# An encoder trunk with routed experts: first three expert passes' rows loaded by token number, a 16-row tile moved up, one entry norm on ScalarE

## The reference, cut to what matters

```python
def hier_moe(h, w_group, w_router, w_gate, w_up, w_down):
    g_probs = softmax(t @ w_group); g_sel = argmax(g_probs)          # 1 of 4 groups
    top_p, top_i = lax.top_k(softmax(e_logits of that group), 2)     # 2 of its 4 experts
    weights = g_w * top_p / sum(top_p)
    hid = silu(t @ w_gate[e]) * (t @ w_up[e]) * gate[e]              # 16 experts, 256 wide
    y = sum over e of hid @ w_down[e]
```

## Time and profile before

| | us |
|---|---|
| median of three runs (lowest, highest) | 1149.74 (1149.23, 1150.93) |
| the profiled execution, device time | 1149.54 |
| its span | 1147.8 |
| TensorE busy | 1060.4 (92%) |
| VectorE / ScalarE / GpSimd busy | 447.5 / 262.4 / 238.5 |
| moved by DMA | 200.88 MB |
| chain that ended last, by engine | PE 79%, DVE 12%, issue 3%, ACT 2%, DMA 2%, POOL 1% |

### The profile page before, as it was taken

The page is one execution under the profiler, slowest core; times in us unless marked ns, Lnnn a source line. Parts: engine busy times, 40 slices in busy tenths (PEclk is TensorE's granted clock), DMA queues, the critical chain, the costliest instruction groups (busy, mean ns, idle before and its releaser), DMA issues.

```text
span 1147.8 us, 16421 instructions
## 1 busy us (share of the span) xinstructions
PE 1060.4 (92%) x6544; PEld 672.0 (59%) x6544; DVE 447.5 (39%) x807; ACT 262.4 (23%) x527; POOL 238.5 (21%) x232
## 2 busy tenths in 40 slices
PE   4999999999999999978999998989998978999992
PEld 4979979989988877753333332454444443333331
DVE  6400314224226540046133125657547745132217
ACT  5132143124224411020011111314214500011111
POOL 5324214305314533003000005510000002000005
PEclk8999999999999999998999998989999997999997
DMA  7232224115115111376799887130003067899946
GB/s 298 74 121 82 66 79 132 55 31 170 55 37 166 37 74 74 147 293 260 283 355 384 354 369 255 49 146 1 1 1 147 1 246 303 333 362 350 381 193 233
DMA packets 34837, 200.88 MB, mean 175 GB/s; under 512 B 4352, under 2 KB 4480, under 8 KB 25808
## 3 DMA queue, kind: packets, MB, share of 16 engines
q1 hardware_dynamic: 21168, 151.26, 34.5%
q10 hardware_dynamic: 8864, 31.63, 7.9%
q0 software_dynamic: 4736, 17.04, 4.0%
HBM read 303.59 MB, written 28.44 MB: 289 GB/s over the span
## 4 chain that ended last, share of the span: by engine, by line
PE 79%; DVE 12%; issue 3%; ACT 2%; DMA 2%; POOL 1%; POOLq 0%; ACTq 0%; DVEq 0%
PE ps L842 30%; PE ps L1076 15%; PE ps L1095 7%; PE ps L967 4%; PE ps L1200 4%; PE ps L1142 3%; PE ps L848 2%; DVE arena L2058 2%; PE ps L1064 2%; DVE arena L2055 2%; PE ps L910 1%; PE ps L1053 1%; PE ps L1014 1%; ACT arena L1510 1%; PE ps L1160 1%
## 5 line engine op out<-in xcount | busy, mean ns | idle before, releaser
L842 PE MATMUL ps<-x_hi,ring_r 128*128 128x264 f32 x1024 | 191.9, 288 | 2.6 <-DVE xT L1550 2.5
L2138 POOL TENSOR_TENSOR ring_r<-ring,ring_r 128x1024 fp32r<-128x1024 f32 x56 | 134.9, 2422 | 266.2 <-ACT ring_r L1292 266.2
L842 PEld LDWEIGHTS ps<-x_hi,ring_r 128*128 128x128 f32 x1024 | 161.1, 190 | 3.3 <-issue 2.9
L1076 PE MATMUL ps<-arena,xT 128*32 128x512 f32 x864 | 158.0, 600 | 0.0
L1076 PE MATMUL ps<-ring,xT 128*32 128x512 f32 x672 | 143.8, 602 | 5.9 <-DVE xT L1550 5.9
L842 PE MATMUL ps<-xT_r,ring_r 128*128 128x264 f32 x512 | 146.6, 286 | 0.0
L1550 DVE TENSOR_TENSOR xT<-ps,gains 128x512 f32<-128x512 f32 (+1 forms) x76 | 47.0, 660 | 186.9 <-PE ps L1064 177.1
L842 PE MATMUL ps<-ring_r,x_hi 128*128 128x512 f32 x320 | 100.5, 395 | 0.0
L842 PEld LDWEIGHTS ps<-xT_r,ring_r 128*128 128x128 f32 x512 | 97.4, 190 | 0.1
L1095 PE MATMUL ps<-arena 128*32 128x512 f32 x624 | 87.3, 595 | 4.3 <-ACT arena L1424 4.3
L1292 ACT ACTIVATE ring_r<-ring 128x1024 fp32r<-128x1024 f32 x56 | 57.9, 1054 | 119.5 <-PE ps L842 70.8
(11 more groups left out here) (264 smaller groups left out, 1573.1 us busy)
## 6 DMA issues: line engine op xcount, KB each, us to landing
arena<-in_w_gu SPq DMA_DIRECT2D x22, 2048.0 KB, 14.9
ring<-in_w_gu SPq DMA_DIRECT2D x20, 2048.0 KB
arena<-in_w_down SPq DMA_DIRECT2D x36, 1024.0 KB
arena<-in_w_gu POOLq DMA_DIRECT2D x18, 2048.0 KB
ring<-in_w_gu POOLq DMA_DIRECT2D x14, 2048.0 KB
arena<-in_w_down POOLq DMA_DIRECT2D x26, 1024.0 KB
ring<-in_w_ret SPq DMA_DIRECT2D x48, 512.0 KB, 3.7
ring<-in_w_ret_out SPq DMA_DIRECT2D x16, 512.0 KB, 4.9
```

The source lines that it names most:

```text
L842: last = mm(dst, a_parts[x], b_parts[y], start=(start and n == 0), stop=(stop and n == 2))
L1076: last = mm(ps[cols, b, :], xgT[:, k % 2, c, cols], by_row(gu(j))[:, c, :], start=(c == 0), stop=(c == KT - 1))
L2138: G.tensor_tensor(w_lo[slot][:, m], w_raw[slot][:, m], w_hi[to][:, m], ALU.subtract).then_inc(lo_made, 1)
```

## The change

- **Rows by token number.** For passes 0, 1 and 2 the one-hot matrices (now three, `slots_of_pass`) are multiplied by a column of token numbers instead of by the rows (`tokens_of`, five products of one column). ScalarE turns the result into integers `token_i`, and GpSimd fetches the 128 rows with one indirect DMA from `token_rows`, a plain copy of the normed rows in device memory that ScalarE stores tile by tile (`store_rows`). The first pass's places are computed from the pairs alone, ahead of the rest of VectorE's steps.
- `tokens_of(1)` stands in the middle of `gate_up(0)`, `tokens_of(2)` behind the turning of pass 1's rows. Pass 0's turned rows are widened by ScalarE in eight pieces (`first_features`).
- GpSimd's order: gather 0, scatters of the first tile, gather 1, further scatters, the singles of pass 0 (`singles_step(0)`), gather 2, the scatters of the last two tiles.
- ScalarE's load of pass 3's rows waits for the scatters and stands behind `results_of(0)`.
- `ROWS_SLOT` is 5, the guessed slots are 0 to 4; pair 5 belongs to pass 3. The table `e_of` is written in two parts. W_Q's first chunk is loaded after the first expert stage.
- The constant products are five behind the logits, five behind the ranks, five behind `tokens_of(0)`.
- **The 16-row tile.** In chunk 3 of the output projection META's products come ahead of tiles 2 and 3, and META is third in layer 0's tile order.
- **Entry.** The last tile is normed by ScalarE instead of VectorE.

```diff
-ROWS_SLOT = 3
-GUESSED = [4, 5, 0, 1, 2]
+ROWS_SLOT = 5
+GUESSED = [0, 1, 2, 3, 4]
+GATHERED = 3
...
+        hot_in = (x_words[:, 3 * D:3 * D + 640], arena[:, LOGITS:LOGITS + 640], arena[:, LOGITS - 2 * D:LOGITS - 2 * D + 640])
+        one_hot = [x.rearrange("p (t s) -> p t s", t=5) for x in hot_in]
...
-        MOE_TILES = [[0, 1, 2, 3, META], [0, 1, 2, 3]]
+        MOE_TILES = [[0, 1, META, 2, 3], [0, 1, 2, 3]]
...
+                    if n == 3:
+                        groups = [groups[0], groups[2], groups[1]]
...
+                def constant_products(n):
+                    for _ in range(n):
+                        mm(ps[:, B_YB, :], ident, con[:, 0:512], start=True, stop=True)
+
+                constant_products(5)
...
-                for _ in range(9):
-                    mm(ps[:, 4, :], ident, con[:, 0:512], start=True, stop=True)
-
-
-                pe.wait_ge(m["slot_ready"], 2)
-                for c in range(2):
+
+                def tokens_of(k):
+                    pe.wait_ge(hot_ready, GATHERED * l + k + 1)
                     for i, t in enumerate(tiles):
-                        last = mm(ps[:, c, :], one_hot[0:rows(t), t, :], xn[0:rows(t), t, 512 * c:512 * c + 512],
+                        last = mm(ps[:, B_TOKENS[k], 0:1], one_hot[k][0:rows(t), t, :], con[0:rows(t), C_TOKEN + t:C_TOKEN + t + 1],
                                   start=(i == 0), stop=(i == len(tiles) - 1))
-                last.then_inc(full[0], 1)
+                    last.then_inc(tokens_made, 1)
+
+                constant_products(5)
+                tokens_of(0)
+                constant_products(5)
                 all_read(pe, t_blocks[l])
 
 
                 def rows_to_features(k):
+                    if k < GATHERED:
+                        pe.wait_ge(rows_gathered[k], 16 * (l + 1))
+                    else:
+                        pe.wait_ge(m[f"x_in{k % 2}"], rows_loaded(k))
                     if k:
-                        pe.wait_ge(m[f"x_in{k % 2}"], rows_loaded(k))
                         round_read(pe, l, B_ROWS, k - 1)
                     for c in range(KT):
                         last = nc.tensor.transpose(ps[:, c // 4, 128 * (c % 4):128 * (c % 4) + 128],
                     if k >= 2:
                         round_read(pe, l, b, k - 2)
                     for c in range(KT):
+                        if k == 0 and c == KT // 2:
+                            tokens_of(1)
                         for cols, j in tiles_of(k):
                             last = mm(ps[cols, b, :], xgT[:, k % 2, c, cols], by_row(gu(j))[:, c, :],
                                       start=(c == 0), stop=(c == KT - 1))
...
 ...
                 rows_to_features(1)
+                tokens_of(2)
...
+                if n == 1:
+                    act.wait_ge(nrm["_r"]["rstd_done"], 5)
+                    act.wait_ge(nrm["_r"]["xn_done"], 4)
+                    nc.scalar.activation(ret_xn[:, TILES5[4], :], h[:, TILES5[4], :], ACT.Copy,
+                                         scale=rstd[:, TILES5[4]:TILES5[4] + 1]).then_inc(nrm["_r"]["xn_done"], 1)
...
+                def store_rows(n):
+                    t = MOE_TILES[l][n]
+                    act.wait_ge(nrm[f"_m{l}"]["xn_done"], n + 1)
+                    act.dma_start(token_rows[128 * t:128 * t + rows(t), :], xn[0:rows(t), t, :]).then_inc(rows_stored, 16)
+
+                for n, t in enumerate(MOE_TILES[l]):
+                    squares(MOE_TILES[l], nrm[f"_m{l}"], moe_junk[l], ready, t)
+                    if n == 2:
+                        for early in range(3):
+                            store_rows(early)
+                for n, t in enumerate(MOE_TILES[l]):
+                    if n + 3 < len(MOE_TILES[l]):
+                        store_rows(n + 3)
                     b = fl.bank(f"LT{l}_{t}")
...
-                fl.wait_full(act, f"X0_{l}")
-                nc.scalar.activation(xg[:, 0, :], flat(ps[:, 0:2, :]), ACT.Copy).then_inc(free[0], 1)
-                act.wait_ge(m["scattered"], 16 * 2 * (5 - l))
-                load_rows(1)
+                def tokens_of(k):
+                    act.wait_ge(tokens_made, GATHERED * l + k + 1)
+                    nc.scalar.activation(token_i[:, l, k:k + 1], ps[:, B_TOKENS[k], 0:1], ACT.Copy).then_inc(tokens_read, 1)
+
+                def first_features():
+                    round_full(act, l, B_ROWS, 0)
+                    for c in range(KT):
+                        last = nc.scalar.activation(xgT[:, 0, c, :], ps[:, c // 4, 128 * (c % 4):128 * (c % 4) + 128], ACT.Copy,
+                                                    scale=gains[:, G_MOE[l], c:c + 1])
+                    last.then_inc(free[B_ROWS], 1)
+
+                tokens_of(0)
+                first_features()
+                tokens_of(1)
                 tanh_of(0)
-                load_rows(2)
+                tokens_of(2)
                 for k in range(1, ROUNDS):
-                    load_rows(k + 2)
+                    if k > 1:
+                        load_rows(k + 2)
                     hidden_of(k - 1)
                     tanh_of(k)
                     results_of(k - 1)
+                    if k == 1:
+                        act.wait_ge(m["scattered"], 16 * 2 * (5 - l))
+                        load_rows(k + 2)
                     if k - 3 in range(len(MOE_TILES[l])):
                         late_weights(MOE_TILES[l][k - 3])
...
+                def slots_of_pass(k, where, numbers):
+
+                    for t in range(nt):
+                        step.done(V_.tensor_scalar(one_hot[k][:, t, :], numbers, where[:, 0, t:t + 1], None, ALU.is_equal))
+                    step.wait()
+                    for t in range(nt):
+                        last = V_.scalar_tensor_tensor(one_hot[k][:, t, :], numbers, where[:, 1, t:t + 1], one_hot[k][:, t, :],
+                                                       ALU.is_equal, ALU.add)
+                    last.then_inc(hot_ready, 1)
+
+                slots_of_pass(0, first_place, iota)
...
-                pool.wait_ge(m["slot_ready"], 1)
-                if l == 0:
-                    pool.wait_ge(s_zeroed, 32 * HEADS)
-                for t in tiles:
-                    r = rows(t)
-                    for c in range(2):
-                        G.indirect_dma_start(slot_rows, bass.IndirectOffsetOnAxis(slot_i[0:r, c, t:t + 1], 0),
-                                             xn[0:r, t, :], None).then_inc(m["scattered"], 16)
-                pool.wait_ge(m["eb_ready"], 1)
+                def gather_rows(k):
+                    pool.wait_ge(tokens_read, GATHERED * l + k + 1)
+                    if k == 0:
+                        pool.wait_ge(rows_stored, 16 * (5 * l + len(tiles)))
+                    if k == 2:
+                        round_full(pool, l, B_ROWS, 0)
+                    G.indirect_dma_start(xg[:, k % 2, :], None, token_rows,
+                                         bass.IndirectOffsetOnAxis(token_i[:, l, k:k + 1], 0)).then_inc(rows_gathered[k], 16)
...
+                def singles_step(k):
+                    if k == 0:
+                        pool.wait_ge(m["eb_ready"], 2)
+                    behind = chosen.pop()
+                    chosen.append({j: single_of(j) for kind, j in PASSES[k] if kind == "pair"})
+                    if chosen[0]:
                         round_full(pool, l, gu_bank(k), k)
-                        singles_weights(load_gate_up, gu_again, k, chosen)
+                        singles_weights(load_gate_up, gu_again, k, chosen[0])
                     if behind:
                         round_full(pool, l, B_YB, k - 1)
                         singles_weights(load_down, down_again, k - 1, behind)
+
+                gather_rows(0)
+                pool.wait_ge(m["slot_ready"], 1)
+                if l == 0:
+                    pool.wait_ge(s_zeroed, 32 * HEADS)
+                for n, t in enumerate(tiles):
+                    if n == 1:
+                        gather_rows(1)
+                    if n == len(tiles) - 2:
+                        singles_step(0)
+                        gather_rows(2)
+                    r = rows(t)
+                    for c in range(2):
+                        G.indirect_dma_start(slot_rows, bass.IndirectOffsetOnAxis(slot_i[0:r, c, t:t + 1], 0),
+                                             xn[0:r, t, :], None).then_inc(m["scattered"], 16)
+                for k in range(1, ROUNDS):
+                    singles_step(k)
                 pool.wait_ge(m["gather_ready"], 1)
                 for j in range(2):
                     pool.wait_ge(m[f"y_out{j}"], results_stored(ROUNDS - 2 - j))

```

174 lines of the change are left out of this document (98 added, 76 removed).

## The result

The changed kernel takes **1161.57 us** (median of 4 runs, 1160.12 to 1163.95), the kernel before 1149.49 beside it: a ratio of **1.0101**, 95% interval 1.0087 to 1.0116, so 12 us slower. The forecast was 1157 (1141 to 1164). The profiled execution took 1160.42, its span 1158.6 (before: 1147.8).

What follows compares the result with a forecast made beforehand. TensorE's own products, one behind the other, mostly bound the kernel. Entry -2.2, T -3.5 and -1.1, G0 -8.2 and -4.5, G1 +6.6 and +4.3, clock +3.0, pass 3's rows +12.8: +7.2, to 1157 us (1141 to 1164).

Steps and rivals of the forecast that it cites:

- Reads free, rows late: Rival: GpSimd's reads ahead of pass 1 cost nothing, pass 3's rows still late; 1157 - 7.7 = 1149; chance 0.10.
- The queue is worse: Rival: with slot 5 and reloads queued, pass 3's loads take 15 us, +5 in either layer, 1167; chance 0.08.
- Entry, -2.2: Kernel start: last tile's norm on ScalarE lets TensorE's first product start 2.2 us earlier, bounds 0 and -2.8.
- T, -3.5 and -1.1: End of the rank products comes 3.5 us earlier in layer 0 (tile order and clock), 1.1 in layer 1 (clock).
- I take 2.2 at the transposed logits: Layer 0: META's products ahead of tiles 2 and 3 bring the transposed logits 2.2 us earlier, bounds 0 and 2.6.
- T to G0, -8.2 and -4.5: From ranks done to start of `gate_up(0)`: gathering rows shortens it by 8.2 us in layer 0, 4.5 in layer 1.
- G0 to G1, +6.6 and +4.3: Start of `gate_up(0)` to `gate_up(1)`: GpSimd's new order, with four reads of `e_of`, adds 6.6 and 4.3 us.
- The clock in pass 1, +1.5 each: TensorE idles some 6 us ahead of `gate_up(1)`, so a lower clock adds 1.5 us in each layer.
- Pass 3's rows, +6.4 a layer: Rows issued behind pass 0's result store land late: +5.0 us wait and +1.4 clock in either layer, +12.8 in all.
- 1144: Rival: pass 3's rows land in time, so their 12.8 us is gone, 1157 - 12.8; chance 0.20.
- 1134: Rival: GpSimd's reads cost almost nothing and pass 3's rows are in time, so the second gather's landing binds; chance 0.12.
- Slot 5's weights are wanted at `gate_up(3)`, about 29 behind G1, issued at 9: Slot 5's load, issued 9 us behind the start of `gate_up(1)` and wanted about 29 behind it, was costed at nothing.

Runs made afterwards that it cites:

- e8: The changed kernel with the last tile's norm given back to VectorE; 1169.07 us, ratio 1.0156 to the kernel before.
- e11: The kernel before with only ScalarE's load of pass 3's rows moved behind results_of(0), both layers; 1167.48 us, ratio 1.0137.
- e10: The changed kernel without the five constant products between the logits and the ranks, both layers; 1168.77 us, ratio 1.0150 to the kernel before.
- e9: The changed kernel with META back behind tiles 2 and 3, VectorE's later norms left where the change put them; 1166.97 us, ratio 1.0139 to the kernel before.
- e4: The changed kernel with SyncE's load of slot 5 held until pass 3's rows have landed; 1157.65 us, ratio 1.0070 to the kernel before.
- e1: The changed kernel with the scatter wait and pass 3's row loads moved ahead of results_of(0); 1150.36 us, ratio 1.0010 to the kernel before.
- e5: The kernel of e1 with later experts' gate-and-up reloads cut to half their columns, slot 5 whole; 1137.68 us, ratio 0.9888 to the kernel before.
- e3: The changed kernel with more scatters and singles_step(0) ahead of gather 1, pass 3's row loads behind tokens_of(2); 1144.03 us, ratio 0.9948 to the kernel before.

## Why the prediction was right in sign, and where its terms were wrong

The direction, the place of the loss and the range were right, but that the time fell into the range is luck in part. Of the stages of the trace, pass 3's rows cost 15.0 us more than their term, and all others together 11.8 less than theirs: 4.7 at G0 to G1, 2.2 at T to G0, 2.0 at the entry and T of layer 0, 1.3 in the clock of pass 1, 1.6 behind. What came is two rivals at once, "Reads free, rows late" (0.10) and "The queue is worse" (0.08), which the list held apart: 1167 less 7.7 is 1159.

- **Entry, -2.2**: -2.7 (e8), in its bounds. Behind it comes a gain that no edit made: the clock rose later in the execution of the kernel before. The first product of line 910 (929 in the changed kernel) starts as follows in the kernel before, in e11, whose entry is the same, and in the changed kernel:

```profile
50.47 0.34 PE L910 MATMUL ps<-ring_r,x_hi 128*128 128x384 f32 x1
```

```profile
49.61 0.34 PE L910 MATMUL ps<-ring_r,x_hi 128*128 128x384 f32 x1
```

```profile
46.89 0.34 PE L929 MATMUL ps<-ring_r,x_hi 128*128 128x384 f32 x1
```

  so the changed kernel is 3.6 ahead there, 0.9 more than at its first product. In 28 to 30 us the granted clock is 0.50 in the kernel before, 0.92 in e11 and 1.00 in the changed kernel.
- **T, -3.5 and -1.1**: -5.0 in layer 0. The clock's part (-1.3, -1.1) is confirmed by e10. The part of the tile, "I take 2.2 at the transposed logits", looks like 3.8, of which 0.9 is the entry's clock and 2.9 the edit's, and for another reason: e9 shows that the tile's place gives nothing and VectorE's norms give it. (In e9 the add of tiles 2 and 3 is 3.9 us ahead of the kernel before, 487.60 against 491.45; so was its first product of line 929 already, at 46.59 against 50.47.)
- **T to G0, -8.2 and -4.5**: -8.5 and -6.4. Gather 0 landed in 5.4 and 5.6 us, where 6.5 and 7.9 were taken; in layer 0 it started 0.8 later than reckoned. (The terms given add up to 18.6 for layer 1, not to the 18.0 of the text.)
- **G0 to G1, +6.6 and +4.3**: +3.3 and +2.9. The step that failed is "then four reads of `e_of` ... I take 0.95, since scatters are landing, so 3.8". They cost nothing on the path. The reads of layer 0, in 536 to 539.3, stand in the view of their line:

```profile
L706 POOLq TENSOR_LOAD <-e_of x4: 292/298/498, 536.8 to 538.7; - x4
```

  They take 0.3 to 0.5 us each and run on GpSimd's sequencer from 536.8 on, beside gather 1 and the scatters that stand ahead of them. POOL's timeline shows the first conditional load behind them ahead of the last two of these scatters, some 0.5 us behind the end of `gate_up(0)` at 540.07, for which it waits.

```profile
539.54 0.96 POOL L2293 DMA_INDIRECT slot_rows<-arena,slot_i  x1 [0.30 <-issue]
540.56 0.05 POOL L699 DMA_DIRECT2D ring<-in_w_gu  x1
540.81 0.86 POOL L2293 DMA_INDIRECT slot_rows<-arena,slot_i  x1 [0.20 <-issue]
540.96 0.05 POOL L699 DMA_DIRECT2D arena<-in_w_gu  x1
```

  Pass 1 then waits for gather 1 (1.46 us) and not for GpSimd. That was the condition of the rival "reads free, rows late".
- **The clock in pass 1, +1.5 each**: +1.7 and 0. In layer 1 TensorE's idle time ahead of G1 was as long, and `gate_up(1)` was still as quick as in the kernel before: G1 to G2 is 11.7.
- **Pass 3's rows, +6.4 a layer**: +14.3 and +13.5. This is the term that decided. The prediction took the landing of 10.2 us from the earlier trace rows, "the queues are full from G1 + 9 on, as at 570". There a slot's 3 MB had long landed and two reloads had been under way for 5.7 us; here slot 5's 3 MB had started 4.0 us and the reloads 0.5 us before the rows. The landing was 16.8. Also the clock behind an 11.5 us wait cost 2.8 where 1.4 were taken (1.1 in the turning, 1.7 in the down product). e11 measures what the earlier trace rows would have given: 8.9 and 8.6, still above 6.4.
- **Behind pass 3** the forecast had nothing but the clock of layer 1's ranks; the trace has 2.7 us of gain: 1.0 there and 1.7 in the attention layer, which the change leaves nearly as it was. The granted clock shows it again: 0.72 in 765 to 777 of the kernel before, 0.86 in the same work of the changed kernel (768 to 780), and 1.00 there in e9. So this too looks like a matter of the executions compared, not of the change.

"What decides is whether pass 3's rows land within 5.4 us of the last issue" was the right question for that wait: in e4 they land 3.9 and 4.5 us behind their issue, and the wait is gone in both layers. But the rivals that followed from it, 1144 and 1134, are refuted as times: e1 has both new waits small and stands at 1150. Their sums took the passes behind as free, and e1 and e5 show that the stream of weights takes back most: of pass 3's 28 us e1 regained 10.5, and e3, with the scatters earlier, 17.6. The remark "Slot 5's weights are wanted at `gate_up(3)`, about 29 behind G1, issued at 9" costed at nothing a stream of weights that e4 shows to be tight.

Of the marks given beforehand, GpSimd's second conditional load came at G0 + 11.2 and not + 16.6, and TensorE's wait ahead of G1 ends with the gather, by which the forecast was to be wrong, and it was, in that term. The wait ahead of pass 3's rows was there, at twice its size.

## What to carry to other kernels

A landing time read elsewhere in the trace holds only for what was in the queues there: list the megabytes issued in the microseconds ahead, and mind that a load with small packets shares packet for packet with weights in large ones. A load that moves from an engine's idle time to behind a store has lost its slack; ask for the first place at which its data exist. And before a saved wait is counted, look whether the DMA engines are full behind it: work that starts 13 us earlier against a stream of weights that starts no earlier gets only part of it back. And before a small gain between two traces is given to an edit, compare the granted clock in the same work: here 0.9 us at the entry and 1.7 in the attention layer came with it.
